# A two-layer decoder trunk on one core: score products in pairs, a new order of events, the first projection group among the input's transposes, and a normalization in two passes

## The reference

```
# layer 0: gated DeltaNet, 8 heads of 128, chunks
qkv, z, beta_logit, a_logit = split(x @ w_in)          # 1024 x 4112
q, k, v = split(silu(causal_conv(qkv, conv_w)))        # 4 taps per channel
q = l2norm(q) * DK**-0.5;  k = l2norm(k)
beta = sigmoid(beta_logit)
g  = -exp(a_log) * softplus(a_logit + dt_bias);  gc = cumsum(g)
decay = exp(gc_i - gc_j) for i >= j, else 0
lmat = strict_lower((k * beta) @ k.T * decay)
u, w = solve(I + lmat, [v * beta, k * beta * exp(gc)])
qk = lower(q @ k.T * decay)
for each chunk:  v_new = u - w @ S
                 o = (q * exp(gc)) @ S + qk @ v_new
                 S = S * exp(g_last) + (k * exp(g_last - gc)).T @ v_new
y = (rmsnorm(o) * norm_g * silu(z)) @ w_out

# layer 1: attention over a window of 128 with sinks, 16 heads, 2 key heads
q, k, v, z = split(x @ w_in);  q = rope(q);  k = rope(k)
p = softmax([q @ k.T * scale within the window, sink])[:-1]
y = ((p @ v) * silu(z)) @ w_out
```

## Time and profile before

| | us |
|---|---|
| median of 3 runs (lowest, highest) | 1060.26 (1059.91, 1060.35) |
| the profiled execution | 1061.88 |
| its span | 1060.1 |
| PE busy | 1028.3 (97%) |
| DVE busy | 703.6 (66%) |
| ACT busy | 498.3 (47%) |
| POOL busy | 219.2 (21%) |

### The profile page before, as it was taken

The page is one execution under the profiler, slowest core; times in us unless marked ns, Lnnn a source line. Parts: engine busy times, 40 slices in busy tenths (PEclk is TensorE's granted clock), DMA queues, the critical chain, the costliest instruction groups (busy, mean ns, idle before and its releaser), DMA issues. The chain is left out here.

```text
span 1060.1 us, 17823 instructions
## 1 busy us (share of the span) xinstructions
PE 1028.3 (97%) x6309; PEld 837.7 (79%) x6309; DVE 703.6 (66%) x1653; ACT 498.3 (47%) x1389; POOL 219.2 (21%) x569
## 2 busy tenths in 40 slices
PE   7999999999999999999999999999999999999996
PEld 6888777878787878888888888888877777777885
DVE  4676767685857576745466767535367778778765
ACT  4655656665657565644353112112155665667000
POOL 1008380828081817270000000000100000000000
PEclk9999999999999999999999999999999999999998
DMA  6231303030313121213114212202001000013201
GB/s 203 62 85 41 96 22 94 21 96 21 78 39 75 42 56 48 48 45 106 40 41 159 79 61 60 70 1 70 20 1 41 21 20 22 21 61 109 90 40 60
DMA packets 83985, 62.67 MB, mean 59 GB/s; under 512 B 32108, under 2 KB 74156, under 8 KB 83896
## 3 DMA queue, kind: packets, MB, share of 16 engines
q1 hardware_dynamic: 49576, 44.68, 14.0%
q10 hardware_dynamic: 34320, 16.84, 6.1%
HBM read 55.18 MB, written 6.32 MB: 58 GB/s over the span
## 5 line engine op out<-in xcount | busy, mean ns | idle before, releaser
L683 PE MATMUL ps<-act_hi,w_hi 128*128 128x512 f32 x512 | 225.9, 441 | 0.0
L683 PE MATMUL ps<-act_hi,w_lo 128*128 128x512 f32 x512 | 201.3, 393 | 0.0
L683 PE MATMUL ps<-act_lo,w_hi 128*128 128x512 f32 x512 | 200.2, 391 | 0.0
L622 POOL TENSOR_TENSOR rank<-inverse,tok 128x60 f32<-128x60 f32 (+24 forms) x248 | 98.1, 395 | 175.0 <-DMA tok<-blocks_in 156.7
L1499 DVE SCALAR_TENSOR_TENSOR tok<-xs,convw,tok 128x512 f32<-128x512 f32 x144 | 112.7, 783 | 13.1 <-ACT xs L1178 11.6
L683 PEld LDWEIGHTS ps<-act_hi,w_lo 128*128 128x128 f32 x512 | 96.1, 188 | 21.5
L683 PEld LDWEIGHTS ps<-act_hi,w_hi 128*128 128x128 f32 x512 | 97.1, 190 | 10.7
L683 PEld LDWEIGHTS ps<-act_lo,w_hi 128*128 128x128 f32 x512 | 97.3, 190 | 9.1
L877 PE MATMUL ps<-wo_hi,act_hi 128*128 128x512 f32 x256 | 101.0, 395 | 1.0 <-DVE wo_lo L1557 1.0
L625 POOL TENSOR_TENSOR inverse<-inverse,rank 128x60 f32<-128x60 f32 (+24 forms) x248 | 96.5, 389 | 19.4
L877 PE MATMUL ps<-wo_lo,act_hi 128*128 128x512 f32 x256 | 100.1, 391 | 0.0
(11 more groups left out here) (268 smaller groups left out, 2192.6 us busy)
## 6 DMA issues: line engine op xcount, KB each, us to landing
w_raw<-in_a_w_in ACTq DMA_DIRECT2D x32, 512.0 KB, 4.2
tok<-in_x SPq DMA_DIRECT2D x8, 512.0 KB, 7.3
decay<-gc_rows SPq DMA_DIRECT2D x8, 512.0 KB, 4.6
tok<-blocks_in SPq DMA_DIRECT2D x32, 128.0 KB, 2.7
xres<-in_x SPq DMA_DIRECT2D x8, 512.0 KB, 3.6
ws_raw<-in_b_w_in SPq DMA_DIRECT2D x16, 256.0 KB, 2.7
z_raw<-in_b_w_in SPq DMA_DIRECT2D x8, 512.0 KB, 3.9
out<-yr SPq DMA_DIRECT2D x8, 512.0 KB, 2.6
```

What stands on the lines that cost most here:

```text
L622: inner.next(pool.tensor_tensor(part, inverse[:, 0:rows, m:m + 1].broadcast_to([P, rows, w]), blocks[:, m:m + 1, m + 1:32].broadcast_to([P ...
L683: mm = pe.matmul(ps[:, g % 2, :], lhs[:, k, :], rhs[:, k, HALF * b:HALF * (b + 1)], start=(i == 0), stop=(i == GROUP - 1))
```

## The change

It has five parts.

1. *First group among the transposes.* Six matmuls of group 0 come between the transposes of tiles 6 and 7, the other 18 ahead of the second half of the gate projection. The split of the first weights moves ahead of the half tile 10 on ACT and DVE, the load of the second ahead of half tile 13. Evacuations, pieces and tanh of groups 0 and 1 come out of the plan and stand among the gates' scalar steps. The gates' first half uses PSUM bank 1. PE enters the plan after 69 matmuls of projection (before 39).
2. *Convolution weights.* One load of 96 rows of 128 and one transpose for three loads of 4 rows of 1024 and 24 transposes.
3. *Scores in pairs.* Four events M in place of eight, each two chunks in one bank (banks 5, 6, 7, 5). Only the last pair waits for DVE. DVE scales the two `k k^T` one by one and both `k q^T` in one instruction.
4. *New tables* of places for all three engines, for all event kinds.
5. *Output stage.* The last tile of each layer is computed half by half, with a signal for each. DVE evacuates and takes statistics half by half. The normalization has two passes in place of three, the first ahead of the wait for the root. In layer 1's last tile the passes and the store are made half by half.

```diff
-AT_PE = {"TQ": [0.6035],
+AT_PE = {"TQ": [0.6027],
-          "M": [0.9953, 1.016, 1.036, 1.057, 1.077, 1.098, 1.118, 1.139],
+          "M": [0.9573, 0.9983, 1.039, 1.08],
...
-INPUT_GATE_BANKS = (0, 4)
+INPUT_GATE_BANKS = (1, 4)
-FETCH_AT = 4
-FIRST = GROUP + 5 * STEP
+FETCH_AT, HIGH_AT, NEXT_AT = 4, 10, 13
+FIRST = 2 * GROUP + 7 * STEP
...
@@ SP
                 sp.dma_start(tok[:, t, :], x[0, t * P:(t + 1) * P, :]).then_inc(s_x[t], 16)
-                if t == 3:
-                    for i, buf in enumerate((qT[0], kT[0], qT[1])):
-                        sp.dma_start(buf[0:CONV_K, :], a_conv[0][:, DM * i:DM * (i + 1)]).then_inc(s_crow, 16)
+            sp.dma_start(conv_rows, a_conv[0].rearrange("k (w p) -> (k w) p", p=P)).then_inc(s_crow, 16)
@@ PE, start
             turn_input(NT // 2 + 2)
+            project(0, 0)
+            project(0, STEP)
             turn_input(NT // 2 + 3)
-            pe.wait_ge(s_crow, 48)
-            for w in range(QKV_TILES):
-                buf = (qT[0], kT[0], qT[1])[w // 8]
-                mm = pe.transpose(ps[:, 2, CONV_K * w:CONV_K * (w + 1)], buf[0:CONV_K, (w % 8) * P:(w % 8 + 1) * P],
-                                  ident[0:CONV_K, 0:CONV_K])
-            mm.then_inc(s_ctr, 1)
+            pe.wait_ge(s_crow, 16)
+            rows = CONV_K * QKV_TILES
+            pe.transpose(ps[:, 2, 0:rows], conv_rows, ident[0:rows, 0:rows]).then_inc(s_ctr, 1)
+            for q in range(2 * STEP, GROUP, STEP):
+                project(0, q)
             pe.wait_ge(s_xlo, 2 * NT)
             project_input_gates(1, 0)
             project_input_gates(1, NK // 2)
-            project(0, 0)
-            project(0, STEP)
+            project(1, 0)
+            project(1, STEP)
@@ PE, scores
+                else:
+                    pe.wait_ge(s_m, NT * h + 2)
+                for i in range(2):
+                    cut = slice((2 * pair + i) * P, (2 * pair + i + 1) * P)
+                    at = 2 * P * i
+                    pe.matmul(ps[:, SCORE_BANKS[pair], at:at + P], kT[h % 3][:, cut], kT[h % 3][:, cut],
+                              start=True, stop=True)
+                    mm = pe.matmul(ps[:, SCORE_BANKS[pair], at + P:at + 2 * P], kT[h % 3][:, cut], qT[h % 3][:, cut],
+                                   start=True, stop=True)
+                mm.then_inc(s_kk, 1)
@@ ACT, input loop
+                if n == HIGH_AT:
+                    high(0)
+                if n == NEXT_AT:
+                    fetch(1)
@@ DVE, matrices
+                both = ps[:, SCORE_BANKS[pair], :].rearrange("p (c a j) -> p c a j", c=2, a=2)
+                for i in range(2):
+                    c = 2 * pair + i
+                    own.next(dve.scalar_tensor_tensor(nT[h % 2][:, c, :], both[:, i, 0, :], sc["ncj"][:, h, c:c + 1],
+                                                      decay[:, c, :], ALU.mult, ALU.mult))
+                cut = slice(2 * pair, 2 * pair + 2)
+                dve.tensor_tensor(aT[h % 2][:, cut, :], both[:, :, 1, :], decay[:, cut, :], ALU.mult).then_inc(s_m, 2)
@@ DVE, out_stage
+                        if t == NT - 1 and half:
+                            dve.wait_ge(s["y"], NT + 1)
...
+                    cuts = [slice(HALF * n, HALF * (n + 1)) for n in range(2)] if last_tile(i, t) else [slice(0, DM)]
+                    for cut in cuts:
+                        own.next(dve.scalar_tensor_tensor(yr[:, q, cut], yr[:, q, cut], mv[:, q, 0:1], lng[:, cut],
+                                                          ALU.subtract, ALU.mult))
                     dve.wait_ge(s["sqrt"], t + 1)
                     own.next(dve.reciprocal(mv[:, q, 3:4], mv[:, q, 3:4]))
                     own.wait()
-                    own.next(dve.tensor_scalar(yr[:, q, :], yr[:, q, :], mv[:, q, 0:1], mv[:, q, 3:4],
-                                               ALU.subtract, ALU.mult))
-                    own.wait()
-                    own.next(dve.tensor_tensor(yr[:, q, :], yr[:, q, :], lng[:, :], ALU.mult))
-                    own.wait()
-                    dve.tensor_tensor(dst, yr[:, q, :], lnb[:, :], ALU.add).then_inc(s["ln"], 1)
+                    for cut in cuts:
+                        dve.scalar_tensor_tensor(dst[:, cut], yr[:, q, cut], mv[:, q, 3:4], lnb[:, cut],
+                                                 ALU.mult, ALU.add).then_inc(s["ln"], 1)
```

More of the change, by code:

```diff
@@ L881, in out_step, with out_last @@
                     mm.then_inc(L[i]["y"], 1)
+            def out_last(i):
+                for half in range(2):
+                    for k in range(NK):
+                        for j in range(PASSES):
+                            lhs = (act_hi, act_hi, act_lo)[j]
+                            rhs = wo[i][j % 2][k]
+                            mm = pe.matmul(ps[:, OUT_BANKS[NT - 1] + half, :], lhs[:, k, (NT - 1) * P:NT * P],
+                                           rhs[:, HALF * half:HALF * (half + 1)],
+                                           start=(k == 0 and j == 0), stop=(k == NK - 1 and j == PASSES - 1))
+                    mm.then_inc(L[i]["y"], 1)
             def out_pair(i, k):
@@ L1517, in piece @@
                                              ALU.add, ALU.mult).then_inc(s_silu, 1)
+            dve.wait_ge(s_cw, 1)
+            for k in range(CONV_K):
+                piece(0, k)
+            dve.wait_ge(s_gtr, 1)
+            lg = ps[:, 3, 0:256].rearrange("p (c j) -> p j c", c=NT)
+            own.next(dve.tensor_tensor(gt[:, 1], lg[:, GH:2 * GH, :],
+                                       bias2[:, 0, :].unsqueeze(2).broadcast_to([P, GH, NT]), ALU.add))
+            own.next(dve.tensor_scalar(gt[:, 0], lg[:, 0:GH, :], -1.0, None, ALU.mult))
@@ new lines, in _ @@
+            own.wait()
+            own.next(dve.tensor_tensor(gt[:, 1], gt[:, 1], lg[:, 3 * GH:4 * GH, :], ALU.add))
+            own.next(dve.tensor_tensor(gt[:, 0], gt[:, 0], lg[:, 2 * GH:3 * GH, :], ALU.subtract))
+            own.wait()
+            dve.tensor_scalar(gt[:, 0], gt[:, 0], 80.0, None, ALU.min).then_inc(s_gd, 1)
+            own.wait()
+            own.next(dve.tensor_scalar(gt[:, 2], gt[:, 1], -1.0, None, ALU.mult))
+            own.wait()
+            dve.tensor_tensor(gt[:, 3], gt[:, 1], gt[:, 2], ALU.min).then_inc(s_gd, 1)
@@ new lines, in _ @@
+            low(1)
+            dve.wait_ge(s_ga, 3)
+            own.next(dve.scalar_tensor_tensor(gt[:, 2], gt[:, 1], 0.0, gt[:, 6], ALU.max, ALU.add))
+            own.next(dve.tensor_scalar(gt[:, 7], gt[:, 4], 1.0, None, ALU.add))
+            own.wait()
+            dve.scalar_tensor_tensor(sc["g"][:, :, :], gt[:, 2], -1.0,
+                                     bias2[:, 1, :].unsqueeze(2).broadcast_to([P, GH, NT]), ALU.mult, ALU.mult)\
+               .then_inc(s_gd, 1)
+            own.next(dve.reciprocal(sc["beta"][:, :, :], gt[:, 7]))
```

185 lines of the change are left out of this document (82 added, 103 removed), and 38 rows, old and new, of tables (AT_ACT, AT_DVE).

## The result

The changed kernel takes 1062.28 us (median of 20 executions, 1060.13 to 1065.14); the kernel before, run beside it on the same chip, 1060.30 (20, 1058.82 to 1063.22). The ratio is 1.0021, 95% interval 1.0013 to 1.0029: 2 us slower, where 7.5 us faster was forecast. The profiled execution took 1064.64 us, 1062.9 of it span.

What follows compares the result with a forecast made beforehand. PE, busy 97% of 1060.1 us, was taken as the bound. 2.7 (start) + 3.0 (scores) - 1.2 (new waits) + 0.5 (layer 1) + 2.5 (tail) = 7.5 us off the median 1060.26: 1052.8, stated as 1053.0, range 1049.5 to 1058.

Steps and rivals of the forecast that it cites:

- Start: Up to the gates' transposes: PE 2.7 us earlier, between 2.0 and 3.3 by weight landing, 1.0 if the clock falls.
- Rival (d): At the start: weights land 2 us later than 17.2 and the clock falls; 1057.2 us, chance 0.07.
- rival (a): Early clock: it falls again, or unprofiled runs never had it low; 1.7 us less gain, 1054.7, chance 0.13.
- Scores: Score products in pairs: most of PE's 3.2 us of waits for DVE go; 3.0 us gained.
- 1.2 for new waits: Head loop: charge of 1.2 us for waits from other moved events, between -3.0 and +3.0.
- Rival (c): Scores: the fourth pair waits in every head; 2.5 us slower, 1062.8, chance 0.05.
- Rival (b): Head loop: the gain at the scores is given back elsewhere; 4.5 us faster, 1055.8, chance 0.17.
- Layer 1's start: First projection of layer 1: PE's 0.5 us wait at L937 goes; 0.5 us gained, between 0 and 1.
- the tail: After PE's last matmul: DVE saves 2.0 us and the store 0.5; sum 2.5, between 1.8 and 2.8.
- waits at the level and solve steps that sum to over 6 us: Sign of being wrong, in the head loop: these waits, 1.8 and 1.2 us before, sum to over 6.
- all four signs of being right: Group 0 at 18.3-19.6, clock 1.00 until 30; score waits under 1 us; L937's first wait gone; DVE's end under 5 us.

Runs made afterwards that it cites:

- e8: The new start alone (groups 0 and 1 outside the plan, convolution weights as in the changed kernel) on the kernel before: 1058.05 us, ratio 0.9972.
- e3: The kernel before with only LATE_TURN[0] moved from -0.0781 to 0.0574, so head 0's events come late: 1065.44 us, ratio 1.0040.
- e12: The kernel before with LATE_TURN[0] at 0.0574, run once more for its trace: 1066.83 us in one execution.
- e7: The scores in four pairs alone, with the changed kernel's four places for M, on the kernel before: 1059.94 us, ratio 0.9987.
- e4: The output stage alone (last tile half by half, two passes, store in two parts) on the kernel before: 1056.86 us, ratio 0.9971.
- e1: The changed kernel with LATE_TURN[0] put back from 0.0574 to -0.0781, so head 0's events come earlier: 1051.34 us, ratio 0.9917.
- e2: The changed kernel with 24 unread 128x512 matmuls ahead of the wait at head 0's first level product: 1058.12 us, ratio 0.9979.
- e6: The changed kernel with the fetch of weight tile 9 moved 20 matmuls (4.4 us) later: 1060.55 us, ratio 0.9997.

## Why the prediction was wrong

**Start: right.** Forecast 2.7 us earlier at the gates' transposes, group 0 at 18.9 and the next projection at 31.2 in place of 33.9. The timeline of PE after, answering to the earlier trace rows:

```profile
18.56 0.47 PE L690 MATMUL ps<-act_hi,w_hi 128*128 128x512 f32 x1 [0.62 <-DVE w_lo L1445]
20.01 1.03 PE L704 MATMUL ps<-ident,tok 128*128 128x128 f32 x8
...
30.19 0.68 PE L732 MATMUL ps<-ident,vT 32*128 32x32 f32 x8
30.80 0.50 PE L690 MATMUL ps<-act_hi,w_hi 128*128 128x512 f32 x1
```

3.1 us, and 2.7 by e8. Rival (d) is out (the weights landed in time), and rival (a) in its first form too: with eight transposes at 20.01 between two stretches of projections, the clock stays at 1.00 from 18.5 to 30.2. In its second form, that executions differ in whether they have the early fall, (a) holds for the kernel before: e3's trace lacks it, e12's has it, and PE is 1.66 us apart. How many of the unprofiled executions have it is not shown.

One reading of the forecast was wrong here, though its conclusion stands. It took the 1.00 of the stretch from 5.0 to 9.4, with transposes only, for full clock. The trace has no clock record before 8.7 us, and a stretch without a record is shown as 1.00. The transposes of the kernel before, from 4.6 to 8.6 and from 8.8 to 10.4 (last columns: busy us, mean ns, idle before), say what the clock was:

```profile
L697 PE MATMUL ps<-ident,tok 128*128 128x128 f32 x19 | 4.3, 421 | 4.6 <-POOL xT L598 4.6
```

```profile
L697 PE MATMUL ps<-ident,tok 128*128 128x128 f32 x14 | 2.0, 287 | 0.0
```

Up to 8.6 us they start 0.21 us apart, from 8.8 on 0.11: PE ran at its lower level first and rose to the full one at 8.7, with nothing but transposes behind it. The changed kernel does the same at the same time. The rule behind the rival, in the Trainium skill, TensorE: Matmul & The Clock Gate, "Part 4: PE-mode transpose", that the clock does not come up for work in transpose mode, does not hold in these traces.

**Scores: more than forecast in the changed tables, less alone.** 3.0 less the 1.2 for new waits made 1.8; PE's progress gives about 3.9 over heads 1 to 7, in which the moved places have their part too (the wait of 1.2 us before `resid` is 0.2 after). Rival (c) is out, since no fourth pair waits. Rival (b) is what e7 shows, and what the new tables avoid.

**Layer 1's start and the tail: right.** 0.5 and 2.5 forecast, 0.6 and 2.6 in the trace, 3.25 together by e4. The last tile after, answering to the earlier trace rows:

```profile
1055.27 0.39 PE L901 MATMUL ps<-wo_hi,act_lo 128*128 128x512 f32 x1
1055.70 0.69 DVE L1744 SCALAR_TENSOR_TENSOR yr<-tok,ps 128x512 f32<-128x512 f32 x1 [3.64 <-PE ps L901]
...
1057.46 1.40 DVE L1755 SCALAR_TENSOR_TENSOR yr<-yr,mv,lng 128x512 f32<-128x512 f32 x2
...
1058.97 1.41 DVE L1761 SCALAR_TENSOR_TENSOR yr<-yr,mv,lnb 128x512 f32<-128x512 f32 x2
1059.75 0.99 SPq L567 DMA_DIRECT2D out<-yr  x2
```

DVE needs 1055.70 to 1060.38, 4.7 us (forecast 4.5 to 4.7), against 6.7 before.

**The step that failed** is one sentence of the forecast: "The plan also moves other events of the head loop by up to a few matmuls, or a piece", priced at "1.2 us for new waits, between -3.0 and +3.0". One event group moved by 19.5 matmuls, not by a few, and it stands at the head of the longest chain of the loop. The forecast priced waits by the rows of PE in the kernel before, where head 0's product does not wait at all: the two waits at L810 in the earlier trace rows are at 179.0 and 341.3 us, of other heads. What was missing is the slack:

```profile
122.28 0.44 DVE L1615 STREAM_TRANSPOSE tok<-xT 32x256 f32<-32x256 f32 x1
```

```profile
123.32 0.69 PE L810 MATMUL ps<-tok,nT 32*32 32x32 f32 x32
```

In the kernel before, the operand was there at 122.7 and PE's product came at 123.3, so the slack was 0.6 us. After the change PE came there 2.8 us sooner (120.5) and the operand 3.8 us later (126.5): 6.6 less the slack of 0.6 is the wait of 6.0. The new start is not to blame for it, since by e8 it brings PE and the operand forward alike. What is to blame is seen against e1, where PE comes at the same time: the scores are 6.2 us later, POOL starts 1.3 sooner behind them, its inverse takes 2.5 longer, and the load goes 2.0 further behind the store. That is 9.4 us at the load, of which e1 had 3.7 in hand: 2.2 before DVE came to the load, 1.5 before PE asked. The forecast named a sign for this, "waits at the level and solve steps that sum to over 6 us", and it came (7.6 us at L821), although all four signs of being right came too.

The second half of the failure is what such a wait costs. With the wait at 6 us and at full clock the whole would have been 8.7 - 6.0 = 2.7 us faster (8.7 is the forecast's sum without its charge of 1.2); e2, with the gap filled, is 2.0 faster than the kernel before. It was the clock behind the wait that turned the sign: e1 to the changed kernel is 10.9 us, of which the gap is 6.05 in the trace and the rest, about 4.9, goes with the clock (7.4 in the traced execution, 13.4 us longer than e1's in span). So where the forecast charged 1.2 us for all new waits, and 3.0 at most, this one cost 10.9 together with its clock. Not all of this went by the same number: the inverse's store was held by the weight fetch (1.3 us by e6), and on POOL the inverse took 36.0 us against 33.5 in e1, the same instructions. In e3, with the same late number in the old order of DVE, it took 32.5, and the wait was 0.4.

What stays open: why the low level lasted 20.5 us in the traced execution of the changed kernel and 3.4 or 6.8 in the others, and which of its executions have which. The mean clocks of the unprofiled ones (0.994, 0.992 and 0.989, with times near 1060.2, 1062 and 1064.5) say that the length varies from one to the next.

## What to carry to other kernels

In a kernel that one engine fills to 97%, the list of waits prices only what is late already; for a change that moves events, follow each moved event to the product of TensorE that needs its result, and write down how much earlier than needed that result comes now. Treat a TensorE wait of some microseconds in the middle as dearer than its length, since the clock may go with it: here 5.6 us cost 10.9. A faster start of the engine at the bottleneck need not make the chains beside it late, where that engine also feeds them: in e8 both came 2.7 us forward. And a column that says full clock where nothing was recorded is checked against the pace of the instructions.
